# Two transformer stacks in one launch: order of the opening transfers, of the vector products beside the first projection, and of the steps in the first attention

## What is computed

```python
for i in range(DEPTH):
    mod = jax.nn.silu(c) @ ada_w[i] + ada_b[i]
    sh_a, sc_a, g_a, sh_f, sc_f, g_f = jnp.split(mod[:, None, :], 6, axis=-1)
    h = rms_norm(x, attn_norm[i]) * (1.0 + sc_a) + sh_a
    ...
        y = sparse_mixer(h, cos, sin, sp_w_in[j], sp_w_out[j], ...)
    ...
    x = x + g_a * y
    h = rms_norm(x, ffn_norm[i]) * (1.0 + sc_f) + sh_f
    x = x + g_f * swiglu(h, ffn_w_gate[i], ffn_w_up[i], ffn_w_down[i])

def sparse_mixer(h, ...):
    mq, mk, mv, nq, nkv, ng = jnp.split(h @ w_in, SPARSE_SPLITS, axis=-1)
    o_moba = moba_attention(...)      # 8 heads, 256 keys
    kc = nsa_compress(...)            # 15 compressed keys and values
    vc = nsa_compress(...)
    o_nsa = nsa_attention(...)        # compressed, selected and window part
    return concat(o_moba, o_nsa) @ w_out
```

## Time and profile before

| what | us |
|---|---|
| median of the runs shown | 1648.61 |
| lowest and highest | 1646.49, 1650.37 |
| the profiled execution | 1653.33 |
| its span | 1651.5 |
| PE busy in it | 1542.3 |
| DVE busy | 1023.3 |
| ACT busy | 760.3 |

### The profile page before, as it was taken

The page is one execution under the profiler, slowest core; times in us unless marked ns, Lnnn a source line. Parts: engine busy times, 40 slices in busy tenths (PEclk is TensorE's granted clock), DMA queues, the critical chain, the costliest instruction groups (busy, mean ns, idle before and its releaser), DMA issues.

```text
span 1651.5 us, 21922 instructions
## 1 busy us (share of the span) xinstructions
PE 1542.3 (93%) x8961; PEld 1230.3 (74%) x8961; DVE 1023.3 (62%) x1599; ACT 760.3 (46%) x1184; POOL 0.2 (0%) x4
## 2 busy tenths in 40 slices
PE   3999989999999789999989999999999998999997
PEld 1667867888877567787768878778787775778786
DVE  2466546666569866556466655676656685366655
ACT  2343535344454434334445554455545543365544
POOL 0000000000000000000000000000000000000000
PEclk9999799999999999999999999999999999999999
DMA  8894056855755847876846655557454663245452
GB/s 300 332 326 155 27 171 220 298 181 183 249 203 178 281 159 250 305 262 212 286 172 230 204 179 189 177 183 256 178 197 158 226 233 128 79 141 186 157 202 89
DMA packets 167908, 336.26 MB, mean 204 GB/s; under 512 B 8184, under 2 KB 109184, under 8 KB 167552
## 3 DMA queue, kind: packets, MB, share of 16 engines
q1 hardware_dynamic: 138880, 230.90, 41.4%
q10 hardware_dynamic: 28928, 103.96, 17.2%
HBM read 333.79 MB, written 1.05 MB: 203 GB/s over the span
## 4 chain that ended last, share of the span: by engine, by line
PE 60%; DVE 24%; ACT 8%; issue 4%; DMA 2%; ACTq 1%; SPq 0%; DVEq 0%
PE ps L1764 11%; PE ps L1765 11%; PE ps L1766 11%; PE ps L1833 10%; DVE wlo L1056 9%; PE ps L1834 5%; ACT whi L607 4%; DVE hbuf L1078 3%; PE ps L1710 3%; ACT hbuf L627 2%; DVE res L1146 1%; DVE work L1144 1%; DMA ring<-in_ada_w_dram 1%; ACTq L371 1%; PE ps L2006 1%
## 5 line engine op out<-in xcount | busy, mean ns | idle before, releaser
L1056 DVE TENSOR_TENSOR wlo<-wraw,whi 128x1024 fp32r<-128x1024 f32 (+1 forms) x420 | 493.2, 1216 | 274.7 <-ACT whi L607 274.3
L607 ACT ACTIVATE whi<-wraw 128x1024 fp32r<-128x1024 f32 (+1 forms) x420 | 418.5, 1044 | 253.6 <-PE ps L1766 138.3
L1833 PE MATMUL ps<-hT,whi 128*128 128x512 f32 x1472 | 525.0, 401 | 2.7 <-DVE hT L1201 2.7
L1834 PE MATMUL ps<-hT,wlo 128*128 128x256 f32 x1472 | 412.6, 280 | 0.0
L1833 PEld LDWEIGHTS ps<-hT,whi 128*128 128x128 f32 x1472 | 276.9, 188 | 82.7 <-issue 9.7
L1834 PEld LDWEIGHTS ps<-hT,wlo 128*128 128x128 f32 x1472 | 278.3, 189 | 0.0
L1764 PE MATMUL ps<-whi,act_hi 128*128 128x512 f32 x560 | 219.7, 392 | 10.0 <-DVE wlo L1056 10.0
L1765 PE MATMUL ps<-wlo,act_hi 128*128 128x512 f32 x560 | 218.1, 390 | 0.0
L1766 PE MATMUL ps<-whi,act_lo 128*128 128x512 f32 x560 | 218.0, 389 | 0.0
L1764 PE MATMUL ps<-whi,hT 128*128 128x512 f32 (+2 forms) x416 | 161.3, 388 | 4.7 <-DVE hT L1201 4.0
L1765 PE MATMUL ps<-wlo,hT 128*128 128x512 f32 (+2 forms) x416 | 158.0, 380 | 0.0
(11 more groups left out here) (223 smaller groups left out, 1381.4 us busy)
## 6 DMA issues: line engine op xcount, KB each, us to landing
wraw<-in_mlp_w_dram SPq DMA_DIRECT2D x96, 1024.0 KB, 5.2
ring<-in_ada_w_dram ACTq DMA_DIRECT2D x80, 1024.0 KB, 6.8
wraw<-in_ffn_w_gate_dram SPq DMA_DIRECT2D x22, 1024.0 KB, 5.3
wraw<-in_ffn_w_up_dram SPq DMA_DIRECT2D x22, 1024.0 KB, 7.0
wraw<-in_ffn_w_down_dram SPq DMA_DIRECT2D x22, 1024.0 KB, 4.9
work<-in_ada_w_dram ACTq DMA_DIRECT2D x16, 1024.0 KB, 15.4
wraw<-in_diff_w_in_dram SPq DMA_DIRECT2D x12, 1024.0 KB, 5.1
wraw<-in_attn_w_qkv_dram SPq DMA_DIRECT2D x12, 1024.0 KB, 5.0
```

The source lines that it names most:

```text
L607: nc.scalar.activation(whi[:, u % 2, part], raw_view(u)[:, part], ACT.Copy).then_inc(hi_ready, 1)
L1056: nc.vector.tensor_tensor(wlo[:, u % 2, part], raw_view(u)[:, part], whi[:, u % 2, part].bitcast(F32), ALU.subtract).then_inc(lo_ready, 1)
L1833: mm(ps[:, bank, :], whi[:, u % 2, c0:c0 + P], hT[:, :, k, :], start=(k == 0), stop=False, skip_group_check=True)
L1834: ins = mm(ps[:, bank, 0:S], wlo[:, u % 2, c0:c0 + P], hT_hi[:, k, :], start=False, stop=(k == KT - 1), skip_group_check=True)
```

## The change

It moves work in the first 220 us of the program. In words:

- ring units 4 to 7 are issued by SP, right behind the first weight unit, and no longer by ACT; that first weight unit waits for one ring unit used, and the second and third weight units wait for none;
- ACT issues ring unit 3 behind the Silu instead of ahead of it, and ring unit 8 behind its half of the norm's columns;
- the 18 small transfers go out between the second and third unit of the panel `in0_0`;
- one vector product moves from the third unit of `in0_2` to the second unit of `in0_1`;
- in the first attention the repeated values are made by two products of 256 columns instead of eight of 64, the halves of the first `out0` units are split earlier, and four of the compressed softmax's DVE operations, its transposes and its copy each come one step later.

```diff
-        IN0_STEPS = {"in0_2": (0, 0, 1, 1), "in0_0": (1, 1, 1, 1), "in0_1": (1, 1, 2, 2)}
+        IN0_STEPS = {"in0_2": (0, 0, 0, 1), "in0_0": (1, 1, 1, 1), "in0_1": (1, 2, 2, 2)}
...
+            def small_rows():
...
                 for i in range(s_["count"]):
-                    if s_["name"] == "in0_2" and i < 3:
-                        sp.wait_ge(ring_used, (1, 4, 6)[i])
+                    if s_["name"] == "in0_2" and i == 0:
+                        sp.wait_ge(ring_used, 1)
+                    if s_["name"] == "in0_0" and i == 2:
+                        small_rows()
                     weight_dma(s_, i)
+                    if s_["name"] == "in0_2" and i == 0:
+                        for r in range(4, FIRST_UNITS):
+                            ring_dma(sp, r)
...
             act.wait_ge(sem("small_params"), 128)
-            ring_fill(4)
+            ring_fill(3)
...
             ins.then_inc(sem("silu_c"), 1)
-            ring_fill(FIRST_UNITS)
+            ring_fill(4)
+            ring_next[0] = FIRST_UNITS
...
             norm_columns((1,))
+            ring_fill(FIRST_UNITS + 1)
             split_unit(1)
...
-                if i in (6, 7, 8, 9):
-                    split_half(by_name["out0"]["base"] + (i - 6) // 2, i % 2)
+                if i in (3, 4, 6, 7):
+                    n = (3, 4, 6, 7).index(i)
+                    split_half(by_name["out0"]["base"] + n // 2, n % 2)
...
-                if i == 8:
+                if i == 9:
                     dve.wait_ge(sem("cmp_turned"), 1)
...
                     link(nc.vector.tensor_reduce(cmp_m[:, :], flat, AX, ALU.add))
-
+                if i == 7:
                     link(nc.vector.tensor_scalar(cmp_m[:, :], cmp_m[:, :], 0.5, None, ALU.max))
...
-                if i in (7, 8, 9, 11):
-                    n = (7, 8, 9, 11).index(i)
+                if i in (5, 8, 9, 11):
+                    n = (5, 8, 9, 11).index(i)
...
-                        for r_ in range(4):
-                            h = 4 * g + r_
-                            ins = mm(ps[:, LINK_BANK, h * HD:(h + 1) * HD], const("spread")[0:NCMP, :], vcr[0:NCMP, g * HD:(g + 1) * HD], start=True, stop=True)
+                        four = vcr[0:NCMP, g * HD:(g + 1) * HD].rearrange("p (r d) -> p r d", r=1).to_broadcast([NCMP, 4, HD])
+                        ins = mm(ps[:, LINK_BANK, 4 * g * HD:4 * (g + 1) * HD].rearrange("p (r d) -> p r d", r=4), const("spread")[0:NCMP, :], four, start=True, stop=True)
...
-                if i == 7:
+                if i == 8:
                     pe.wait_ge(sem("cmp_p"), 1)
```

More of the change, by code:

```diff
@@ L500, in _ @@
             sp.dma_start(pos_i[:, :], positions[0].rearrange("(t p) -> p t", p=P), allow_slow_non_contiguous=True).then_inc(xl, 16)
-            g = sem("gains_landed")
-            rows = [moba_q_norm[0:1], moba_k_norm[0:1], nsa_q_norm[0:1], nsa_k_norm[0, 0:1], nsa_k_norm[0, 1:2],
-                    nsa_k_norm[0, 2:3], diff_q_norm[0:1], diff_k_norm[0:1]]
-            for n, row in enumerate(rows):
-                sp.dma_start(gains[:, n, :], row.to_broadcast([P, HD])).then_inc(g, 16)
-            sp.dma_start(gains2[:, 0, :], attn_q_g_2[0:1].to_broadcast([P, HD2])).then_inc(g, 16)
-            sp.dma_start(gains2[:, 1, :], attn_k_g_2[0:1].to_broadcast([P, HD2])).then_inc(g, 16)
-            sp.dma_start(gain_o[:, :], diff_out_norm[0:1].to_broadcast([P, HD2])).then_inc(g, 16)
-            for n in range(4):
-                sp.dma_start(lam_p[:, n, :], diff_lambda[0, n:n + 1].to_broadcast([P, HD])).then_inc(g, 16)
-            w2 = nsa_cmp_w2[0].rearrange("s (k p) d -> s p k d", p=P)
-            sp.dma_start(w2k[:, :, 0, :], w2[0]).then_inc(g, 16)
-            sp.dma_start(w2k[:, :, 1, :], w2[0]).then_inc(g, 16)
-            sp.dma_start(w2v[:, :, :], w2[1]).then_inc(g, 16)
+            def small_rows():
+                g = sem("gains_landed")
+                rows = [moba_q_norm[0:1], moba_k_norm[0:1], nsa_q_norm[0:1], nsa_k_norm[0, 0:1], nsa_k_norm[0, 1:2],
+                        nsa_k_norm[0, 2:3], diff_q_norm[0:1], diff_k_norm[0:1]]
+                for n, row in enumerate(rows):
+                    sp.dma_start(gains[:, n, :], row.to_broadcast([P, HD])).then_inc(g, 16)
+                sp.dma_start(gains2[:, 0, :], attn_q_g_2[0:1].to_broadcast([P, HD2])).then_inc(g, 16)
+                sp.dma_start(gains2[:, 1, :], attn_k_g_2[0:1].to_broadcast([P, HD2])).then_inc(g, 16)
+                sp.dma_start(gain_o[:, :], diff_out_norm[0:1].to_broadcast([P, HD2])).then_inc(g, 16)
+                for n in range(4):
+                    sp.dma_start(lam_p[:, n, :], diff_lambda[0, n:n + 1].to_broadcast([P, HD])).then_inc(g, 16)
+                w2 = nsa_cmp_w2[0].rearrange("s (k p) d -> s p k d", p=P)
+                sp.dma_start(w2k[:, :, 0, :], w2[0]).then_inc(g, 16)
+                sp.dma_start(w2k[:, :, 1, :], w2[0]).then_inc(g, 16)
+                sp.dma_start(w2v[:, :, :], w2[1]).then_inc(g, 16)
             def weight_dma(s_, i):
```

## The result

| what | before | changed |
|---|---|---|
| median of the runs taken side by side, us | 1649.49 (4 runs) | 1632.02 (4 runs) |
| lowest and highest | 1646.49, 1654.57 | 1629.78, 1637.24 |
| ratio | | 0.9895, 95% interval 0.9861 to 0.9930 |
| the profiled execution, its span | 1653.33, 1651.5 | 1631.8, 1630.0 |
| PE's mean granted clock in it | 0.973 | 0.977 |

The changed kernel is 17.5 us faster, where 10.1 were forecast. It is within the range, at its lower end. A second measurement gave 0.9891 (0.9875 to 0.9906).

What follows compares the result with a forecast made beforehand. ACT's issuing was taken to bound the start, and PE the panels after it. Terms -10.0 + 0 + 0 + 1.5 - 0.5 - 1.1 = -10.1 took 1648.6 to 1638.5 us, range 1632 to 1644.5.

Steps and rivals of the forecast that it cites:

- What bounded the start: Up to 28 us, ACT issuing transfers ahead of the norm's squares bounds the start, not PE and not data.
- the tail: From normalised input to first projection product, 7.44 us (34.96 to 42.40), forecast to stay as it is.
- Part 1: Opening, first half of the vectors sooner: transposes of x start at 24.9 instead of 34.96, -10.0 us (-13.5 to -6.5).
- The weighing of the rule: Moving issues to SP: the skill's rule makes it worth nothing, near 1648; the profile row of 11.27 us was followed.
- My reading of the blockade: Opening, 10 to 15 us: small transfers, mostly 128 rows of 256 bytes, hold up both SP's and ACT's queues.
- Parts 2 and 3: Second half and first weight units in time, 0 us, at worst +2; small transfers sent later, 0 us.
- The first queue's sum: SP's early queue: six and a half MB and one unit of ACT's from 16 us on end near 38.
- Part 4: Vector product moved from `in0_2` to `in0_1`: a third double unit in a row adds a ring wait, +1.5 us (0 to +4).
- rival C: Supply: panels starting ten us sooner need 350 GB/s; at 325 it costs +4.6, giving 1643.1; chance 0.13.
- Part 5: First attention: repeated values in two products, -0.5, and four small DVE operations behind step 7's maxima, -1.1.
- rival A: First attention: less waiting in step 7 may spare the 10.20 us half-clock stretch, 5.1 us, giving 1633.4; chance 0.15.

Runs made afterwards that it cites:

- e_open: Changed kernel with the first attention's code as before, so only the opening and the vector-product table are changed; ratio 0.9935 to the kernel before.
- g_eight: Changed kernel with one edit undone: the repeated values are eight products of 64 columns again; ratio 0.9915 to the kernel before.
- f_fill: Changed kernel with 21 products added whose results nobody reads, put around PE's waits at the first attention; ratio 0.9899 to the kernel before.
- f_steps: Changed kernel with the table of vector products set back to that of the kernel before; ratio 0.9879 to the kernel before.
- g_spread: Changed kernel with a third table of vector products, no two double units in a row; ratio 0.9897 to the kernel before.
- e_small: Kernel before with only the 18 small transfers moved, between the second and third unit of `in0_0`; ratio 0.9970.
- experiment 7: Two runs of the changed kernel with other tables of vector products: the table of before, ratio 0.9879, and a third table, 0.9897.

## Why the prediction was right, and where it was short

**What bounded the start: right.** In the first profile every mark of the opening but one came within 0.5 us: first vector product 10.74 (11), squares 11.25 (11.5), normalised input 18.8 (18.6), ring unit 3 seen at 22.85 (23.0), transposes of x at 24.70 (24.9), led by ring data. The first projection product came at 30.73, not 32.4: the tail shrank from 7.44 to 6.03, 1.2 of it since PE's transposes took 1.97 at the full clock, where the 3.15 of before were run mostly at half. That was a term that I had kept as it was.

That close a hit is in part luck. The opening is the same in seven profiles (changed twice, `e_open`, `g_eight`, `f_fill`, `f_steps`, `g_spread`), and its transposes of x start anywhere from 22.51 to 26.96, around the 24.9 forecast and inside its bounds of 21.4 and 28.4.

**Part 1, -10.0:** -10.3 at the transposes of x, -11.7 at the first projection product, and -10.75 behind the second half. Held in this profile, and over the runs `e_open`, the opening with the new table, brings 10.0 in total and 7.8 at equal clock, where parts 1 and 4 together say 8.5.

**The weighing of the rule.** The Trainium skill's sentence on issuing engines (DMA: Bandwidth & Descriptors, "Issuing engines are not separate DMA queues"; the sequencer's time is "usually small relative to the DMA itself") would have given nothing. Three issues took 10.11 us of ScalarE in `e_small`, and four took 6.98 of SyncE in the changed kernel, where it holds up no arithmetic. The row decided, rightly. My reading of the blockade named only the small transfers; for the 11.27 us they are not needed, since 10.11 stay without them.

**Parts 2 and 3, 0:** held. The first queue's sum was short: four weight units of 0.81 MB, four ring units and ScalarE's one are 8.5 MB and end near 39, not 38; nobody waited for it. The second weight unit landed late (ScalarE waited 8.57 us for it, until 37.87), and DVE wanted it only at 45. The small transfers went out from 41.08 to 52.5, and the seventh weight unit at 52.53, where 54 had been the latest.

**Part 4, +1.5:** the waits for the ring grew by 1.35 us in the first profile (2.87 for 1.52) and by more in the second; 8.14 of 10.75 us were left at the first scores. Some of that loss is the clock: 3.4 us at 0.50, from 114.7 to 118.1, stand there in the changed kernel and not in the one before. The waits are right in kind. That the kernels that start sooner wait longer for the same units (experiment 7) is what rival C, supply, says; the runs cannot tell the two apart, and part of what was gained at the start may be lost to it.

**Part 5, -1.6:** its own worth is -1.4 ± 0.6 over the runs and -1.2 to -1.7 in the profiles. The sum is right, its two terms are not. The repeated values save 0.87, not 0.5; the 2.25 us were read as run at the half clock, but it fell only at 161.8, 1.6 us after their start. The four small operations save less than the 1.1: the wait of 2.14 us ahead of step 7's transposes is gone, but three shorter ones, 1.8 us together, stand in its place, which `e_open` with the old code does not have.

```profile
171.85 0.85 PE L2016 MATMUL ps<-cst,work 128*128 128x128 f32 x6 [0.53 <-ACT work L797]
176.00 0.84 PE L2016 MATMUL ps<-cst,work 128*128 128x128 f32 x6 [0.92 <-ACT work L797]
179.82 0.85 PE L2016 MATMUL ps<-cst,work 128*128 128x128 f32 x6 [0.36 <-ACT work L797]
```

That is 0.3 us less waiting. One term too small and one too large make up for each other.

**The step that failed** is the one behind the sum: that everything else stays. At equal clock the changed kernel is 11.1 us faster by the fit, 7 to 11 with the doubt in the clock's price, and the forecast said 10.1. The other 6.6 us go with a mean clock of 0.9787 in place of 0.9717, and that was rival A, at 0.15, with one spared stretch of 10.20 us at half (-5.1). That less time is spent at 0.50, as A has it, is what happened; that less waiting in step 7 is the reason is not shown. By two profiles each, the time at 0.50 falls from 90.3 and 86.9 to 75.0 and 58.2 us, 22.0 in the mean, which fits the clock of the runs. Of these, 15.6 lie in the attention (26.4 and 15.2 before, 6.9 and 3.5 after), 7 us at 0.46, and 3.4 ahead of it and 3.0 behind. The 7 us and the 6.6 are two prices of much the same thing and are not to be added. I had held against A that the first stretch came with no idle time at all, which is true and was no argument, since its place is not fixed: four profiles of the old attention's code show 26.4, 21.3, 15.2 and 8.1 us. One profiled execution shows one hand of several, and I reckoned with its stretches in the attention as if they belonged to the kernel.

The Trainium skill (TensorE: Matmul & The Clock Gate, "What's actually happening") says that the low clock is the default and activity releases it. The rows here show 0.50 beside a PE that is busy all the time, as in the earlier trace rows and in `f_fill`, and filling gaps brought nothing; the rule alone does not account for these stretches.

**What stays open:** why the mean clock rises. Each attention edit raised it by 0.002 to 0.004, the opening by 0.0023 ± 0.0011, `e_small` not at all. Fewer small products (`g_eight`) and a shift in time are both possible, and the kernel's clock in the attention varies so much between executions that ten profiles leave room for either. That the added clock is the cause of the 6.6 us, and not another thing's companion, rests on the attention's two lines, where the work is the same and only the time at 0.50 differs; for the rest of the kernel it is argued from the scatter.

## What to carry to other kernels

An engine that issues large transfers ahead of its own arithmetic pays for whatever stands in the queue: look for "issue" idle time in front of a first operation whose data have landed, and give the issues to an engine that has nothing to compute. Transfers of many short rows go behind the first large ones, not ahead of them, once nobody needs them early. When one profiled execution shows long stretches at half the clock, take the mean clock of many executions before you price them, and compare two versions at equal clock as well as in total. Give the price of the clock with its doubt: here two ways to it lie at 0.29 and at 0.38 to 0.46 us for a microsecond at 0.50.

## What the runs showed of the hardware

- A queue with short rows in it holds up the other engine's issue as well: 5.30 us for one issue that takes 0.37 otherwise, both queues ending within 0.02 us of each other.
- With only large transfers ahead, three issues of 1 MiB take 10.11 us, near the 8.1 to 8.6 us that their data take at 365 to 390 GB/s (an estimate).
- Same work, same DVE and ACT busy time, and the attention takes from 57.13 to 68.82 us by the time that TensorE spends at 0.50; a microsecond there costs 0.38 to 0.46, not 0.5. Part of it falls into waits: PE is busy for 5.38 of the 6.90 us from 196.5 on.
- Executions of one kernel differ in mean granted clock from 0.965 to 0.978; by the slope of the fit that is 12 us.
- TensorE ran at 0.50 for 13.6 us while it was busy all the time; with the same code in another execution only 3.4 us stood there.
